# RWKV projection: GpSimd makes the low parts of the odd mixed rows, and mixed rows have four buffers instead of two

## The chip, the cores and the metric

One core of one Trainium2 chip runs the whole program. The metric is the device time of one execution in microseconds; of several executions the median is given.

## The reference

One inference step of a four-layer decoder with D = 1024, for a prompt of 512 tokens and 8 samples of 8 tokens (576 token columns in all). The mixers of the layers are RWKV-7, forgetting attention, a short convolution, and RWKV-7 again; each is followed by a convolutional FFN. The part that matters is the head of the RWKV mixer: six mixtures of the normed row and the row before it, each multiplied by a weight matrix.

```python
x_prev = jnp.concatenate([shift[:, None].astype(xn.dtype), xn[:, :-1]], axis=1)
dx = x_prev - xn
mix = lambda c: xn + dx * mu[c]
r = mix(0) @ w_rkv[0]
k = mix(2) @ w_rkv[1]
v = mix(3) @ w_rkv[2]
w_log = -jax.nn.softplus(-(w0 + jnp.tanh(mix(1) @ w1) @ w2).astype(f32)) - 0.5
iclr = jax.nn.sigmoid((a0 + (mix(4) @ a1) @ a2).astype(f32))
g = jax.nn.sigmoid(mix(5) @ g1) @ g2
```

## The kernel before

Activations lie transposed: 128 channels on the partitions, 576 token columns; the 1024 channels are 8 such rows. A matrix product is made in three matmuls with operands split into a high part (fp32r) and a low part: high times high, low times high weight, high times low weight (L408 to L410, `chunk_mm`). A chunk is 8 rows of one output tile: 8 rows x 2 halves of 288 columns x 3 = 48 matmuls.

Weights come in chunks by DMA from the queue of SyncE into four `raw` buffers. ScalarE copies a chunk to its high part `wh` (`split_hi`, L383) as soon as TensorE is done with the chunk two before; VectorE subtracts for the low part `wl` (`split_lo`, L390). Both have two buffers.

In an RWKV layer (layers 0 and 3) the mixed rows are made on the way. The projections stand in `MIX` in the order r, k, v (8 chunks each), g1, w1, a1 (one chunk each). For each of the six, a set of 8 rows is made:

- VectorE makes the mixed row `xt` = `dx` * mu + `xn` (L764, "mix" below). `xt` has two buffers, so row k waits until row k-2 has its low part.
- ScalarE copies `xt` to the high part `xh` (L779). It waits until TensorE has used this row of the set before (semaphore `a_row`).
- VectorE subtracts `xt` - `xh` into the low part `xl` (L758, "low part" below).

On VectorE the order is mix 0, mix 1, low 0, mix 2, low 1, and so on to mix 7, low 6, low 7 (`mix_rows_dve`). `mixes` (L781) puts the set of the next projection ahead of the last chunk of the present one: on VectorE and ScalarE the set comes first, then the weight split for the chunk after the next, then ScalarE's copy of the finished tile out of PSUM. TensorE (`mix_pe`, L839) waits in the first chunk of a projection, row by row, for the count of `s_xl`.

Engines run their instructions in the order written; semaphores hold them to each other. GpSimd does nothing in this stretch: its program for the layer (`a_pool`, L1717) begins with a wait for the last projection, after which `rwkv` runs the recurrence. There GpSimd's subtractions and products (L1188 to L1197, L1650) run beside VectorE's (L962, L964, L1097, L1102); in the FFN GpSimd copies a few columns (L635) beside VectorE's L390 and L595.

The address range of `xt` starts at `misc`, where the FFN has its `gate` and `conv` buffers and the recurrence its own.

Of the kernel before, what the change touches and what calls it, by code (L numbers as in the profile page):

```python
# [13 lines left out]
F32 = mybir.dt.float32  # L14
F32R = mybir.dt.float32r
I32 = mybir.dt.int32
ALU = mybir.AluOpType
ACT = mybir.ActivationFunctionType
# [4 lines left out]
KD = D // P  # L23
# [3 lines left out]
T = TP + TSN  # L27
# [65 lines left out]
MIX = [("r", 0), ("k", 2), ("v", 3), ("g1", 5), ("w1", 1), ("a1", 4)]  # L93
# [21 lines left out]
def build_program(nc, I, O, mixers=MIXERS):  # L115
# [3 lines left out]
    with ctx:  # L119
        m = Map((nc.sbuf_base + 31) // 32 * 32)  # L120

        def at(name, shape, dt, offset):
            return nc.alloc_sbuf_tensor_at(name, [P] + list(shape), dt, offset=offset)

        def sb(name, shape, dt=F32):
            return at(name, shape, dt, m.take(4 * int(np.prod(shape))))

        def sem(name):
            return ctx.enter_context(nc.semaphore(name))
# [4 lines left out]
        xh, xl = sb("xh", [KD, T], F32R), sb("xl", [KD, T], F32R)  # L134
# [4 lines left out]
        par = sb("par", [NPAR])  # L139
# [8 lines left out]
        misc = f.at  # L148
# [6 lines left out]
        co = at("co", [KF, 2 + 2 * NS], F32, f.take(4 * KF * (2 + 2 * NS)))  # L155
        cs = at("cs", [KF, 2 * NS], F32, f.take(4 * KF * 2 * NS))
        rs2 = at("rs2", [T], F32, f.take(4 * T))
        assert f.at <= nc.sbuf_usable_end, (f.at, nc.sbuf_usable_end)
        xt = at("xt", [2, T], F32, misc)

        b = Map(big)
# [31 lines left out]
        def flat3(t):  # L194
# [6 lines left out]
        xn, dx = at("xn", [KD, T], F32, at_xn), at("dx", [KD, T], F32, at_dx)  # L201
        la = at("la", [T], F32, at_rstd)
        sg = at("sg", [T], F32, a.take(4 * T))
# [10 lines left out]
        zz, csum, pprev, pinv, kraw, kn = (  # L214
            at("a_" + k, [n, NCK, CT], F32, a1.take(4 * n * TP)) for k, n in
            (("zz", 2), ("csum", 1), ("pprev", 1), ("pinv", 1), ("kraw", 1), ("kn", 1)))
# [33 lines left out]
        def pst(b, lo=0, hi=T):  # L250
            return ps[:, tile_cols(b) + lo:tile_cols(b) + hi]
# [9 lines left out]
        s_xt, s_xh, s_xl = sem("s_xt"), sem("s_xh"), sem("s_xl")  # L261
# [13 lines left out]
                "vu nc nx nb sex src ptp pts vs pn stp ogs oxh oxl").split())  # L275

        (a_ld, a_xn, a_dx, a_sh, a_w2, a_z, a_k1, a_k2, a_zz, a_kn, a_sg, a_cs, a_cm, a_kr, a_kv, a_kk, a_ex,
         a_kh, a_bb, a_ar, a_bk, a_rk, a_bo, a_bon, a_p1, a_cx, a_xe, a_cu, a_ue, a_cs2, a_s, a_co, a_oe,
         a_m, a_e, a_d, a_qx, a_qxt, a_qX, a_qxb, a_qU, a_qus, a_qo, a_qvq, a_quq, a_qs, a_qad, a_qmu,
         a_g, a_gd, a_gb, a_gc, a_gs, a_gq, a_gr, a_gl, a_ge, a_gt, a_ga, a_gh, a_kb, a_row, a_out) = (  # L280
            sem("a_" + k) for k in (
                "ld xn dx sh w2 z k1 k2 zz kn sg cs cm kr kv kk ex kh bb ar bk rk bo bon p1 cx xe cu ue cs2 s co oe "
                "m e d qx qxt qX qxb qU qus qo qvq quq qs qad qmu "
                "g gd gb gc gs gq gr gl ge gt ga gh kb row out").split())

# [4 lines left out]
        plan, c, n = {}, 0, 0  # L290
# [3 lines left out]
        for layer, (kind, idx) in enumerate(mixers):  # L294
# [10 lines left out]
            for name, nch, ntile in names:  # L305
                ph = Ph()
# [8 lines left out]
                c, n = c + nch, n + ntile  # L315
        NCHUNK = c
        n_norm, row0, raw_norm, in_place = {}, {}, {}, {}
# [29 lines left out]
        def turns(n):  # L347

            return n // 2 + 1
# [41 lines left out]
                              ALU.subtract).then_inc(s_lo, 1)  # L391

        def chunk_mm(pe, c, n, rh, rl, k0=0, nk=CH, first=True, last=True, i=0, cstep=0, nstep=0, row_ready=None,
                     row_used=None, between=None):

            pe.wait_ge(s_lo, i * cstep + c + 1)
            if first:
                pe.wait_ge(s_ev[n % 2], i * (nstep // 2) + turns(n))
            for k in range(nk):
                if between is not None:  # L400
                    between(k)
                if row_ready is not None:
                    pe.wait_ge(row_ready[0], row_ready[1] + k)
                for a in range(2):
                    out = pst(n % 2, a * HT, (a + 1) * HT)
                    rhs_h, rhs_l = rh[:, k0 + k, a * HT:(a + 1) * HT], rl[:, k0 + k, a * HT:(a + 1) * HT]
                    w_h, w_l = wh[:, c % SPL, k], wl[:, c % SPL, k]
                    pe.matmul(out, w_h, rhs_h, start=(first and k == 0), stop=False)  # L408
                    pe.matmul(out, w_h, rhs_l, start=False, stop=False)  # L409
                    mm = pe.matmul(out, w_l, rhs_h, start=False, stop=(last and k == nk - 1))  # L410
                if row_used is not None and k < nk - 1:
                    mm.then_inc(row_used, 1)
            mm.then_inc(s_mm, 1)
# [130 lines left out]
        def first_chunk(pe, c, n, q, e):  # L544

            def between(k):
                if k == CH // 2:
                    last_squares(pe, q - 1)

            chunk_mm(pe, c, n, xh, xl, row_ready=(s_gl, KD * e + 1), between=between)  # L550
# [201 lines left out]
        def mix_rows_dve(dve, layer, j, n):  # L752

            r0 = row0[layer, "mix"] + n * KD

            def lo(k):
                dve.wait_ge(s_xh, r0 + k + 1)
                dve.tensor_tensor(xl[:, k], xt[:, k % 2], xh[:, k].bitcast(F32), ALU.subtract).then_inc(s_xl, 1)  # L758

            for k in range(KD):  # L760
                if k >= 2 or n:
                    dve.wait_ge(s_xl, r0 + k - 1)
                mu = PC["mu", j] + MIX[n][1] * KD + k
                dve.scalar_tensor_tensor(xt[:, k % 2], dx[:, k], par[:, mu:mu + 1], xn[:, k],  # L764
                                         ALU.mult, ALU.add).then_inc(s_xt, 1)
                if k >= 1:
                    lo(k - 1)
            lo(KD - 1)

        def mix_rows_act(act, layer, j, n):  # L770
            r0 = row0[layer, "mix"] + n * KD
            for k in range(KD):
                act.wait_ge(s_xt, r0 + k + 1)
                if n and k < KD - 1:
                    act.wait_ge(a_row, ((len(MIX) - 1) * j + n - 1) * (KD - 1) + k + 1)
                elif n:
                    before = plan[layer, MIX[n - 1][0]]
                    act.wait_ge(s_mm, before.c0 + before.nch)
                act.activation(xh[:, k], xt[:, k % 2], ACT.Copy).then_inc(s_xh, 1)  # L779

        def mixes(eng, layer, j, mix_rows, chunk):  # L781

# [46 lines left out]
        def key_squares(pe, j, k):  # L829

            pe.wait_ge(a_k2, KD * j + k + 1)
            for blk in range(5):
                at_ = 16 * blk + 2 * k
                for h in range(2 if blk < 4 else 1):
                    mm = pe.matmul(bank(7)[64 * h:64 * h + 64, at_:at_ + 2],
                                   sq[:, k % 2, blk * P + 64 * h:blk * P + 64 * h + 64], hs2(), start=True, stop=True)
            mm.then_inc(a_kn, 1)

        def mix_pe(pe, layer, j, n):  # L839
            name = MIX[n][0]  # L840
            ph = plan[layer, name]
            r0 = row0[layer, "mix"] + n * KD
            for k in range(ph.nch):
                chunk_mm(pe, ph.c0 + k, ph.n0 + k, xh, xl, row_ready=(s_xl, r0 + 1) if k == 0 else None,
                         row_used=a_row if k == ph.nch - 1 and n + 1 < len(MIX) else None)
                if name == "k" and k:
                    key_squares(pe, j, k - 1)
                if name == "v" and k == 0:
                    key_squares(pe, j, KD - 1)
# [40 lines left out]
        def after(eng, s, v):  # L890

            if v > 0:
                eng.wait_ge(s, v)
# [3 lines left out]
        t3, bb, kh = zz0, zz1, kn  # L897
# [279 lines left out]
        def prep_pool(pool, B, G, k):  # L1177
# [36 lines left out]
            k=("et", "m6", 2, "copy", "", "m1", ("p16", "vst")),  # L1214
# [270 lines left out]
        def rwkv(eng, j, inv_step, chain_part, prep_piece, first, seq, states_in=None):  # L1485

            fns = (inv_step, chain_part, prep_piece)
            for k in range(NPREP):
                prep_piece(eng, Bat(j, 0), None, k)
            first(eng, Bat(j, 0))  # L1490
            for c in range(KD + 1):
                half(eng, *fns, Bat(j, c), Bat(j, c - 1) if c else None, Bat(j, c + 1) if c < KD else None,
                     Bat(j, c - 2) if c >= 2 else None, states_in if c == KD - 1 else None)
            seq(eng, j, Bat(j, KD, 7))
# [220 lines left out]
            res_dve(dve, plan[layer, "out"], 1, norm_behind(layer, "out"), None, True)  # L1715

        def a_pool(pool, layer, j):  # L1717
            pool.wait_ge(s_mm, plan[layer, MIX[-1][0]].c0 + 1)
            pool.wait_ge(a_ld, 64 * (j + 1))
            rwkv(pool, j, inv_pool, no_chain, prep_pool, first_none, seq_pool)  # L1720
# [912 lines left out]
```

## Time and profile before

| | before |
|---|---|
| median of three runs | 3803.13 us (3798.8 to 3804.16) |
| profiled execution | 3803.17 us, its span 3801.3 us |
| busy share of the span | TensorE 95%, weight loads 89%, VectorE 48%, ScalarE 37%, GpSimd 11% |
| TensorE's granted clock, mean | 0.975 of full speed |

PE is TensorE's matmuls, PEld its weight loads, DVE is VectorE, ACT ScalarE, POOL GpSimd, SP SyncE. A row of a timeline has the start in us from the start of the span, the duration in us, then engine, line, operation, out<-in and shape; like neighbours are merged (x2). In brackets stands how long the engine was idle before and which instruction ended that. Matmuls are pipelined: one starts before the end of the one ahead, so the pace is read from the starts.

### The profile page before, as it was taken

What the parts mean: (1) busy time and instruction counts of PE and PEld (TensorE: products, weight loads), DVE (VectorE), ACT (ScalarE), POOL (GpSimd) and SP (SyncE); (2) the same over time, 40 slices, a digit from 0 to 9 for tenths busy, and PEclk for the clock granted to TensorE, in tenths of its full rate; (3) what the DMA queues carried; (4) which work ended last, traced back from release to release, by engine and by line L of the source; (5) the groups of instructions that cost most, each with busy time, mean ns of one, the idle gap of its engine ahead of it and who ended that gap; (6) DMA issues with size and microseconds to landing.
All of it is one profiled execution on the core that took longest, in us unless ns stands there. A gap on an engine that the chain in (4) does not pass through costs nothing.

```text
span 3801.3 us, 95974 instructions
## 1 busy us (share of the span) xinstructions
PE 3598.1 (95%) x41213; PEld 3367.6 (89%) x41213; DVE 1830.8 (48%) x2739; ACT 1403.5 (37%) x2390; POOL 424.3 (11%) x570
## 2 busy tenths in 40 slices
PE   6979989999999989899999999999798899999999
PEld 5968888999999955699999999999798787899999
DVE  3465544555245644355533445552435655455532
ACT  2345542444222533244422224442234454244421
POOL 0012211111000000011100101110000332211100
PEclk8989989999999999999999999999899899999999
DMA  3210001222222378422222222222222000122222
GB/s 121 73 45 4 4 25 67 83 83 84 79 83 80 115 281 301 162 82 81 83 86 84 84 73 85 79 81 86 87 73 67 14 4 26 38 80 83 83 81 80
DMA packets 95940, 314.75 MB, mean 83 GB/s; under 512 B 18946, under 2 KB 20226, under 8 KB 94866
## 3 DMA queue, kind: packets, MB, share of 16 engines
q1 hardware_dynamic: 87410, 285.25, 22.5%
q10 hardware_dynamic: 8224, 24.88, 1.7%
q8 instruction: 257, 4.21, 0.5%
q14 instruction: 49, 0.40, 0.0%
HBM read 297.30 MB, written 12.79 MB: 82 GB/s over the span
## 4 chain that ended last, share of the span: by engine, by line
PE 88%; DVE 6%; ACT 3%; issue 2%; DMA 0%; POOL 0%; ACTq 0%; SPq 0%; DVEq 0%; POOLq 0%
PE ps L408 22%; PE ps L410 22%; PE ps L409 22%; PE ps L1342 6%; DVE xt L764 2%; PE ps L538 2%; DVE xl L758 1%; PE ps L904 1%; PE ps L461 1%; PE ps L1421 1%; PE ps L1911 1%; PE ps L1512 1%; PE ps L2010 1%; PE ps L1946 1%; PE ps L1966 1%
## 5 line engine op out<-in xcount | busy, mean ns | idle before, releaser
L408 PE MATMUL ps<-xh,wh 128*128 128x288 f32 x4720 | 1418.5, 301 | 67.6 <-DVE xl L758 66.8
L409 PE MATMUL ps<-xl,wh 128*128 128x288 f32 x4720 | 1397.4, 296 | 0.0
L410 PE MATMUL ps<-xh,wl 128*128 128x288 f32 x4720 | 1392.5, 295 | 0.0
L408 PEld LDWEIGHTS ps<-xh,wh 128*128 128x128 f32 x4720 | 889.1, 188 | 83.0 <-issue 51.2
L383 ACT ACTIVATE wh<-raw 128x1024 fp32r<-128x1024 f32 x415 | 439.2, 1058 | 1249.4 <-PE ps L410 1241.2
L410 PEld LDWEIGHTS ps<-xh,wl 128*128 128x128 f32 x4720 | 893.5, 189 | 0.0
L409 PEld LDWEIGHTS ps<-xl,wh 128*128 128x128 f32 x4720 | 891.6, 189 | 2.0
L390 DVE TENSOR_TENSOR wl<-raw,wh 128x1024 fp32r<-128x1024 f32 x415 | 508.3, 1225 | 611.1 <-ACT wh L383 608.5
L408 PE MATMUL ps<-hh,wh 128*128 128x288 f32 x1536 | 464.5, 302 | 0.0
L410 PE MATMUL ps<-hh,wl 128*128 128x288 f32 x1536 | 457.0, 298 | 0.0
L409 PE MATMUL ps<-hl,wh 128*128 128x288 f32 x1536 | 450.0, 293 | 0.0
L409 PEld LDWEIGHTS ps<-hl,wh 128*128 128x128 f32 x1536 | 294.5, 192 | 2.0
L408 PEld LDWEIGHTS ps<-hh,wh 128*128 128x128 f32 x1536 | 290.5, 189 | 2.8 <-issue 0.7
L410 PEld LDWEIGHTS ps<-hh,wl 128*128 128x128 f32 x1536 | 289.8, 189 | 0.0
L1342 PE MATMUL ps<-m,m 64*64 64x64 f32 x5952 | 238.4, 224 | 14.0 <-issue 7.5
L1342 PEld LDWEIGHTS ps<-m,m 64*64 64x64 f32 x5952 | 202.4, 136 | 50.0 <-issue 44.2
L635 POOL COPY co<-gate 128x2 f32 x96 | 113.9, 1186 | 1046.9 <-DVE gate L448 916.0
L448 DVE TENSOR_TENSOR gate<-ps,rstd 128x512 f32<-128x512 f32 (+1 forms) x176 | 72.5, 454 | 293.1 <-PE ps L410 291.8
L492 ACT ACTIVATE sq<-x 128x576 f32<-128x576 f32 (+1 forms) x64 | 44.0, 687 | 341.9 <-DVE x L509 160.8
L1361 ACT ACTIVATE m<-ps 128x256 f32<-128x256 f32 x272 | 105.6, 389 | 132.4 <-PE ps L1342 128.8
L509 DVE TENSOR_TENSOR x<-x,ps 128x576 f32<-128x576 f32 (+1 forms) x64 | 48.3, 754 | 201.0 <-PE ps L410 201.0
L448 DVE TENSOR_TENSOR conv<-conv,rstd 128x512 f32<-128x512 f32 x192 | 79.5, 456 | 67.8 <-ACT conv L578 67.5
(333 smaller groups left out, 4870.7 us busy)
## 6 DMA issues: line engine op xcount, KB each, us to landing
raw<-in_w SPq DMA_DIRECT2D x415, 512.0 KB, 3.4
kp<-in_cache_k SPq DMA_DIRECT2D x64, 512.0 KB, 5.7
vp<-in_cache_v SPq DMA_DIRECT2D x64, 512.0 KB, 5.8
rkv<-in_wkv ACTq DMA_DIRECT2D x2, 2048.0 KB, 10.0
out_wkvs<-rkv ACTq DMA_DIRECT2D x2, 2048.0 KB, 7.2
x<-in_x ACTq DMA_DIRECT2D x1, 2304.0 KB, 13.0
out_k<-qk ACTq DMA_DIRECT2D x1, 2304.0 KB, 7.0
out_v<-vg ACTq DMA_DIRECT2D x1, 2304.0 KB, 13.0
```

Source lines behind the costliest of these rows:

```text
L383: act.activation(wh[:, c % SPL], raw[:, c % RAWS], ACT.Copy).then_inc(s_hi, 1)
L390: dve.tensor_tensor(wl[:, c % SPL], raw[:, c % RAWS], wh[:, c % SPL].bitcast(F32), ALU.subtract).then_inc(s_lo, 1)
L408: pe.matmul(out, w_h, rhs_h, start=(first and k == 0), stop=False)
L409: pe.matmul(out, w_h, rhs_l, start=False, stop=False)
L410: mm = pe.matmul(out, w_l, rhs_h, start=False, stop=(last and k == nk - 1))
L448: op = dve.tensor_tensor(out(part), src(part), tok(r, part), ALU.mult)
L509: dve.tensor_tensor(row, row, pst(n % 2).rearrange("p (o t) -> p o t", o=1), ALU.add)\
L538: mm = pe.matmul(pst(STAT, a * HT, (a + 1) * HT), ones, sq[:, (j + 1) % 2, a * HT:(a + 1) * HT], start=False, stop=False)
L635: pool.tensor_copy(co[:, bass.ds(i * 2 + u, 1), 0:2], one(gate[:, u, GS - 2:GS]))
L764: dve.scalar_tensor_tensor(xt[:, k % 2], dx[:, k], par[:, mu:mu + 1], xn[:, k], ALU.mult, ALU.add).then_inc(s_xt, 1)
L1342: mm = pe.matmul(bank(bk + part)[to, at_:at_ + CT], operand(B, left, p)[r], mview("ist")[r] if right == "ist" else operand(B, right, p)[r] ...
L1361: act.activation(sl[to][:, of], half_of(bk, part), ACT.Copy).then_inc(a_e, 1)
```

## The change

GpSimd makes the low parts of rows 1, 3, 5 and 7 of each set and counts them on a new semaphore `a_xo`; VectorE makes those of rows 0, 2, 4 and 6 and counts them on `s_xl`. VectorE's order is now mix 0, mix 1, low 0, mix 2, mix 3, low 2, and so on to mix 6, mix 7, low 6. `xt` has four buffers, so mix k waits for the low part of row k-4, of whichever engine. TensorE waits for each row on the semaphore of the engine that makes it.

```diff
-        xt = at("xt", [2, T], F32, misc)
+        xt = at("xt", [4, T], F32, misc)
...
         def chunk_mm(pe, c, n, rh, rl, k0=0, nk=CH, first=True, last=True, i=0, cstep=0, nstep=0, row_ready=None,
-                     row_used=None, between=None):
+                     row_used=None, between=None, mixed=None):
...
+                if mixed is not None:
+                    pe.wait_ge((s_xl, a_xo)[k % 2], mixed // 2 + k // 2 + 1)
...
             def lo(k):
                 dve.wait_ge(s_xh, r0 + k + 1)
-                dve.tensor_tensor(xl[:, k], xt[:, k % 2], xh[:, k].bitcast(F32), ALU.subtract).then_inc(s_xl, 1)
+                dve.tensor_tensor(xl[:, k], xt[:, k % 4], xh[:, k].bitcast(F32), ALU.subtract).then_inc(s_xl, 1)
 
             for k in range(KD):
-                if k >= 2 or n:
-                    dve.wait_ge(s_xl, r0 + k - 1)
+                if k % 2:
+                    after(dve, a_xo, r0 // 2 + k // 2 - 1)
+                else:
+                    after(dve, s_xl, r0 // 2 + k // 2 - 1)
                 mu = PC["mu", j] + MIX[n][1] * KD + k
-                dve.scalar_tensor_tensor(xt[:, k % 2], dx[:, k], par[:, mu:mu + 1], xn[:, k],
+                dve.scalar_tensor_tensor(xt[:, k % 4], dx[:, k], par[:, mu:mu + 1], xn[:, k],
                                          ALU.mult, ALU.add).then_inc(s_xt, 1)
-                if k >= 1:
+                if k % 2:
                     lo(k - 1)
-            lo(KD - 1)
+
+        def mix_rows_pool(pool, layer, j, n):
+
+            r0 = row0[layer, "mix"] + n * KD
+            for k in range(1, KD, 2):
+                pool.wait_ge(s_xh, r0 + k + 1)
+                pool.tensor_tensor(xl[:, k], xt[:, k % 4], xh[:, k].bitcast(F32), ALU.subtract).then_inc(a_xo, 1)
...
-                act.activation(xh[:, k], xt[:, k % 2], ACT.Copy).then_inc(s_xh, 1)
+                act.activation(xh[:, k], xt[:, k % 4], ACT.Copy).then_inc(s_xh, 1)
...
-                chunk_mm(pe, ph.c0 + k, ph.n0 + k, xh, xl, row_ready=(s_xl, r0 + 1) if k == 0 else None,
+                chunk_mm(pe, ph.c0 + k, ph.n0 + k, xh, xl, mixed=r0 if k == 0 else None,
                          row_used=a_row if k == ph.nch - 1 and n + 1 < len(MIX) else None)
...
         def a_pool(pool, layer, j):
+            for n in range(len(MIX)):
+                mix_rows_pool(pool, layer, j, n)
             pool.wait_ge(s_mm, plan[layer, MIX[-1][0]].c0 + 1)
```

## Rows read from the trace of the kernel before

**Rows 1.** the page's costliest groups: line, engine, operation | busy us, mean ns | idle before

```profile
L408 PE MATMUL ps<-xh,wh 128*128 128x288 f32 x4720 | 1418.5, 301 | 67.6 <-DVE xl L758 66.8
```

**Rows 2.** TensorE's waits, 37 to 262 and 2720 to 2965 us: total, times, longest

```profile
PE ps L408 <- DVE xl L758: 33.1, 24, 18.9
...
PE ps L408 <- DVE xl L758: 33.7, 23, 19.8
```

**Rows 3.** timeline of TensorE at 224 to 232 us: start us, us, instruction

```profile
224.76 0.29 PE L409 MATMUL ps<-xl,wh 128*128 128x288 f32 x1
224.90 0.29 PE L410 MATMUL ps<-xh,wl 128*128 128x288 f32 x1
227.87 0.37 PE L408 MATMUL ps<-xh,wh 128*128 128x288 f32 x1 [2.69 <-DVE xl L758]
```

**Rows 4.** timeline of VectorE, the set of projection g1

```profile
211.77 1.54 DVE L764 SCALAR_TENSOR_TENSOR xt<-dx,par,xn 128x576 f32<-128x576 f32 x2
213.34 0.76 DVE L758 TENSOR_TENSOR xl<-xt,xh 128x576 fp32r<-128x576 f32 x1
214.13 0.82 DVE L764 SCALAR_TENSOR_TENSOR xt<-dx,par,xn 128x576 f32<-128x576 f32 x1
214.87 0.75 DVE L758 TENSOR_TENSOR xl<-xt,xh 128x576 fp32r<-128x576 f32 x1
...
222.48 1.59 DVE L758 TENSOR_TENSOR xl<-xt,xh 128x576 fp32r<-128x576 f32 x2
224.26 1.23 DVE L390 TENSOR_TENSOR wl<-raw,wh 128x1024 fp32r<-128x1024 f32 x1 [0.19 <-ACT wh L383]
```

**Rows 5.** timeline of ScalarE, the same set

```profile
212.62 1.42 ACT L779 ACTIVATE xh<-xt 128x576 fp32r<-128x576 f32 x2 [1.49 <-DVE xt L764]
...
223.19 1.04 ACT L383 ACTIVATE wh<-raw 128x1024 fp32r<-128x1024 f32 x1
```

**Rows 6.** stretch of one set: length, busy PE PEld DVE ACT POOL, clock, DMA, GB/s

```profile
225.40:239.00 13.60, 9.31 (x48) 7.78 (x48) 13.09 (x18) 7.57 (x10) 0.00 (x0) 0.87 0.11 39
```

**Rows 7.** timeline of VectorE at 281 us, in the recurrence

```profile
280.81 0.68 DVE L1097 SCALAR_TENSOR_TENSOR a_kn<-a_zz,rkv 128x512 f32<-128x512 f32 x1
...
281.74 1.42 DVE L1102 SCALAR_TENSOR_TENSOR a_zz<-rkv,par,a_kn 128x512 f32<-128x512 f32 x1
```

**Rows 8.** timeline of GpSimd over the same stretch

```profile
280.97 1.65 POOL L1191 TENSOR_TENSOR a_zz<-a_kraw,a_zz 128x512 f32<-128x512 f32 x1 [3.48 <-DVE a_kraw L1090]
282.70 1.59 POOL L1195 TENSOR_TENSOR bst<-a_zz,a_pinv 128x512 f32<-128x512 f32 x1
284.25 1.27 POOL L1197 TENSOR_TENSOR kst<-a_kn,a_pinv 128x512 f32<-128x512 f32 x1
```

**Rows 9.** lines L964 and L962: duration in ns, least, median, most

```profile
L964 DVE TENSOR_TENSOR rkv<-rkv x18: 691/693/1520, 535.6 to 3294.2; 128x512 f32<-128x512 f32 x18
...
L962 DVE TENSOR_TENSOR rkv<-rkv,ps x18: 677/686/689, 534.9 to 3293.5; 128x512 f32<-128x512 f32 x18
```

**Rows 10.** timeline at 581 us, VectorE's L964 and GpSimd's L1650

```profile
580.98 1.52 DVE L964 TENSOR_TENSOR rkv<-rkv 128x512 f32<-128x512 f32 x1
...
580.91 1.04 POOL L1650 TENSOR_TENSOR uq<-a_kraw,msk 128x512 f32<-128x512 f32 x1
...
581.91 1.49 POOL L1650 TENSOR_TENSOR uq<-a_kraw,msk 128x512 f32<-128x512 f32 x1
```

**Rows 11.** timeline of the FFN at 710 us

```profile
709.52 1.23 DVE L390 TENSOR_TENSOR wl<-raw,wh 128x1024 fp32r<-128x1024 f32 x1 [0.18 <-ACT wh L383]
...
709.58 1.21 POOL L635 COPY co<-gate 128x2 f32 x1 [10.66 <-DVE gate L448]
...
710.66 0.83 DVE L595 SCALAR_TENSOR_TENSOR conv<-gate,par,conv 128x592 f32<-128x592 f32 x1
```

**Rows 12.** GpSimd's first subtraction (line L1188) and the timeline before it

```profile
L1188 POOLq MODIFY_POOL_CONFIG  x2: 6/6/6, 252.8 to 252.9; - x2
...
258.05 1.36 POOL L1188 TENSOR_TENSOR a_pprev<-a_csum,a_zz 128x512 f32<-128x512 f32 x1 [5.16 <-DVE a_csum L1070]
```

More of the change, by code:

```diff
@@ L277, in build_program @@
         (a_ld, a_xn, a_dx, a_sh, a_w2, a_z, a_k1, a_k2, a_zz, a_kn, a_sg, a_cs, a_cm, a_kr, a_kv, a_kk, a_ex,
-         a_kh, a_bb, a_ar, a_bk, a_rk, a_bo, a_bon, a_p1, a_cx, a_xe, a_cu, a_ue, a_cs2, a_s, a_co, a_oe,
+         a_kh, a_bb, a_ar, a_bk, a_xo, a_rk, a_bo, a_bon, a_p1, a_cx, a_xe, a_cu, a_ue, a_cs2, a_s, a_co, a_oe,
          a_m, a_e, a_d, a_qx, a_qxt, a_qX, a_qxb, a_qU, a_qus, a_qo, a_qvq, a_quq, a_qs, a_qad, a_qmu,
@@ L281, in build_program @@
             sem("a_" + k) for k in (
-                "ld xn dx sh w2 z k1 k2 zz kn sg cs cm kr kv kk ex kh bb ar bk rk bo bon p1 cx xe cu ue cs2 s co oe "
+                "ld xn dx sh w2 z k1 k2 zz kn sg cs cm kr kv kk ex kh bb ar bk xo rk bo bon p1 cx xe cu ue cs2 s co oe "
                 "m e d qx qxt qX qxb qU qus qo qvq quq qs qad qmu "
```

## The prediction

> **What bounds the kernel now.** I read the page's costliest groups first: TensorE is the long engine, and in front of L408, the first matmul of a row, it stands idle for 67.6 us, of which the waits for `xl` of L758 are 66.8 us [rows 1]. Then TensorE's waits in the two stretches that hold the change, one for each RWKV layer: 33.1 and 33.7 us [rows 2]. The longest of each, 18.9 and 19.8 us, is the norm ahead of the first row, which the change doesn't touch. So 14.2 and 13.9 us remain, and these rows count less than what is lost: a matmul is recorded as 0.29 us but starts 0.13 us after the one before [rows 3], so a row of six takes 0.80 us, a chunk of 48 matmuls 6.4 us.
>
> The timeline of VectorE shows why there is a wait. In one set (eight rows) VectorE runs mix, low part, mix, low part without a pause: 213.34 to 214.87 is one row, 1.52 us, against TensorE's 0.80. Counted from its first mix (211.77), a set ends its last low part at 12.30 us, and the weight split behind it at 13.72 us [rows 4]. ScalarE, with 0.7 us a row, follows [rows 5]. Three of the six projections have one chunk only, and there one set follows on the other every 13.6 us while TensorE needs 6.4. Such a set begins with a wait of TensorE, 2.69 us at 227.87 [rows 3], and in such a stretch the granted clock is 0.87 of full speed [rows 6]: part of it runs at the lower of the two levels. That costs little, as TensorE waits for rows anyway.
>
> **The change part by part.** *Removed:* 4 of 16 VectorE instructions per set, 48 of the 96 low parts, each 0.75 us. *Added:* 48 GpSimd subtractions of 128x576, no new DMA, and a wait of VectorE on GpSimd's row k-4.
>
> If VectorE and GpSimd did not disturb each other, a pair of rows would cost VectorE 0.73 + 0.73 + 0.75 = 2.2 us and some wait instead of 3.04. But they do. GpSimd's L1191 started at 280.97, in VectorE's L1097 (280.81 to 281.49), and ended at 282.62, 1.13 us after the end of L1097. VectorE's L1102, issued at 281.74, ended 0.54 us after that, at 283.16. GpSimd's L1195, started at 282.70, ended 1.13 us later still [rows 7, 8]. One after the other, then: whoever comes second does nothing until the first has ended. An undisturbed one took 1.27 us [rows 8]. The same VectorE line shows both prices: L964, with two SBUF operands, takes 693 ns, and 1520 ns where it meets GpSimd; L962, with one operand in PSUM, never takes over 689 ns [rows 9]. There GpSimd's operation ended at 581.95, L964 at 582.50, and GpSimd's next, begun at 581.91, took 1.49 us instead of 1.04 [rows 10]. Mix (`dx`, `xn`), low part (`xt`, `xh`) and weight split (`raw`, `wh`) all read two SBUF tensors. I take the exclusion as holding for all of them.
>
> Price of one GpSimd subtraction: no row has 576 columns. By columns (576/512 = 1.125) the hold is 1.13 x 1.125 = 1.27 us, and an undisturbed one 1.43 us. Bounds: below, 0.90 us (L1650 from 582.50 to 583.40, with a broadcast operand [rows 10]) x 1.125 = 1.02; above, the whole 1.65 us of L1191 [rows 8] x 1.125 = 1.86, should writing fp32r cost GpSimd more. I take 1.27, as L1191 and L1195 have the same two full operands. VectorE's rest after a release is 0.54 x 1.125 = 0.61.
>
> Who gets in first? In the FFN, GpSimd's L635, of two columns, waited from 709.58 through VectorE's split (709.52 to 710.75) and was done at 710.79, ahead of VectorE's L595, issued at 710.66 [rows 11]. So GpSimd gets its turn between two VectorE instructions.
>
> Now one set, from its first mix at 0 (ScalarE 0.69 us per high part): mix 0 to 0.82, mix 1 to 1.55, low 0 to 2.33, mix 2 from 2.25 to 3.06. Row 1's high part is ready at 2.28, only 0.05 us ahead of the turn at 2.33; I let GpSimd miss it, get the one at 3.06 and hold to 4.33 (if it gets the first, the walk below gives 10 us a layer, 3823). Mix 3, held back, ends at 4.94; low 2 runs from 4.86. From here each pair repeats: mix 0.73, GpSimd 1.27, rest of a mix 0.61, low 0.67 = 3.28 us a pair, against 3.04 now. Low 6 ends at about 12.3; low 7, on GpSimd from 12.3 and undisturbed, at 13.7, 1.4 us later than now. ScalarE's weight part is ready by 13.4, but VectorE's split now waits for low 7: 13.7 + 1.08 = 14.8, 1.1 us later than now. Each set delays TensorE by one or the other, so a layer loses between 6 x 1.1 = 6.6 and 6 x 1.43 = 8.6 us. Walking the four queues set by set gave 1.5, 1.5, 0.9, 1.4, 1.0 and 1.0: 7.3. Two layers: **+14.5 us**.
>
> Costed at nothing: the four buffers. A mix now starts 0.035 us behind the low part it waits for (213.34 + 0.76 to 214.13 [rows 4]); with four it waits for row k-4, done a pair before, and the 0.035 is in the pairs above. If row k-4's part on GpSimd is late, mix k stands, with VectorE's later low parts and weight splits queued behind. TensorE's wait per row in place of a count: nothing. GpSimd's own queue: its copy for the recurrence comes behind the last set and wants the last projection anyway. GpSimd's first subtraction brings two MODIFY_POOL_CONFIG of 6 ns, which stood at 252.8, ahead of a wait that ended at 258.05, not behind it [rows 12]; they will now stand at the program's start, under 40 us of idle. Were they behind the wait, up to 5.2 us once. The lower clock: a row takes 1.6 us at half speed, against 1.64 between rows, so at most some tenths at each set's last row, under 4 us in all, in the range.
>
> Sum against the profiled execution: its own time is 3803.17 us (span 3801.3), and the median of the three runs is 3803.13, the same. 3803.2 + 14.5 = 3817.7, say 3818.
>
> **The rivals.** *No exclusion for these operations* (faster). The place is VectorE's pair of rows: 2.24 us, GpSimd's 1.43 beside it. The same walk ends the last low part at 10.5 instead of 12.3 and the weight split at 11.4 instead of 13.7, 1.8 to 2.35 us a set, 12.5 a layer: 3803 - 25 = 3778. For it: no row shows a mix beside a GpSimd operation. Against: the same kinds of instruction do exclude each other [rows 7 to 10]. The point that decides is the hold of GpSimd: 0.73 + hold + 0.61 + 0.67 = 3.04 at 1.03 us; below it, faster.
>
> The Trainium skill, Advanced Engine Details and Errata, Mode Summary, notes the blocking only for GpSimd against VectorE instructions in a two-port mode, and the Trainium skill, VectorE: DVE Perf Modes, The perf-mode tier table, gives fp32 `tensor_tensor` no such mode; by that the time would be the 3778 of this rival. The GPSIMD Details of the first page count VectorE instructions with two SBUF inputs in as well, and the 1520 ns are on the side of this second line.
>
> *A short hold.* Each us of hold is worth 24 us a layer (24 pairs): at 1.02 it is 7.3 - 24 x 0.25 = 1.3 a layer, 3806: no change that can be measured.
>
> *GpSimd is slower at fp32r.* At 1.86 us: 7.3 + 24 x 0.59 = 21.5 a layer, 3846. Against: the hold of 1.13 repeats to 0.01 in rows 7 and 8.
>
> **How the numbers follow.** Exclusion with a hold of about 1.1 to 1.5: 0.60, 3810 to 3830, likeliest 3818. Short hold, 3803 to 3810: 0.13. Slow GpSimd, 3830 to 3846: 0.09. No exclusion, about 3778: 0.18. About 0.2% (7.6 us) is what a measurement here can tell from no change. Faster 0.18, same 0.13, slower 0.69. The range, 3802 to 3846, leaves out the case of no exclusion and little else, 0.2.
>
> **What would show it.** Right: VectorE's mixes and low parts fall into two durations, undisturbed (0.75 to 0.82) and about 1.9 to 2.0 us for the mix that meets GpSimd; GpSimd's subtractions take 1.4 to 2.0 us, the wait in them included; a set lasts about 13.7 us to its last low part; TensorE's waits name `xl` of GpSimd. Wrong: mixes that stay at 0.82 us beside GpSimd, sets of 10.5 us, or a GpSimd hold below 1.03 us; a first set later by some 5 us would mean the configuration is behind the wait.

## The result, and the profile after

| | before | after |
|---|---|---|
| median of nine runs each | 3802.77 us (3798.8 to 3804.16) | 3813.11 us (3806.32 to 3820.27) |
| ratio of the times | 1 | 1.003, 95% interval 1.0022 to 1.0039 |
| profiled execution, its span | 3803.17 us, 3801.3 us | 3814.71 us, 3812.9 us |
| TensorE's granted clock, mean | 0.975 | 0.977 |

The changed kernel is slower by 0.2 to 0.4%: 8.4 to 14.8 us by the interval, 10.3 by the medians, 11.5 between the two profiled executions. The lines moved a little: mix is now L768, VectorE's low part L760, GpSimd's L778, ScalarE's high part L789, the first matmul of a row L410.

The page, first the busy shares of the engines, then the groups that answer to [rows 1] (busy us, mean ns | idle time before and what ended it):

```profile
PE 3599.5 (94%) x41213; PEld 3363.0 (88%) x41213; DVE 1837.6 (48%) x2691; ACT 1403.1 (37%) x2390; POOL 508.5 (13%) x618
...
L410 PE MATMUL ps<-xh,wh 128*128 128x288 f32 x4720 | 1422.4, 301 | 75.6 <-DVE xl L760 52.0
...
L778 POOL TENSOR_TENSOR xl<-xt,xh 128x576 fp32r<-128x576 f32 x48 | 86.0, 1792 | 563.4 <-ACT xh L789 563.4
```

VectorE has 48 instructions fewer for the low parts and still 48% of the span: what it gave away it spends blocked. TensorE stands idle before the first matmul of a row for 75.6 us, 8.0 more than in [rows 1]. In the first of the two stretches (37 to 266 us) its waits now have two names:

```profile
PE ps L410 <- DVE xl L760: 25.6, 12, 18.9
PE ps L410 <- POOL xl L778: 11.3, 16, 0.9
```

Beside the norm's 18.9 that is 6.7 + 11.3 = 18.0 us, against 14.2 in [rows 2].

The cause stands in the set of one projection with one chunk. VectorE's timeline (start, us, instruction), answering to [rows 4]:

```profile
232.15 1.53 DVE L768 SCALAR_TENSOR_TENSOR xt<-dx,par,xn 128x576 f32<-128x576 f32 x2
233.71 0.76 DVE L760 TENSOR_TENSOR xl<-xt,xh 128x576 fp32r<-128x576 f32 x1
234.38 2.69 DVE L768 SCALAR_TENSOR_TENSOR xt<-dx,par,xn 128x576 f32<-128x576 f32 x2
237.00 0.75 DVE L760 TENSOR_TENSOR xl<-xt,xh 128x576 fp32r<-128x576 f32 x1
237.67 2.70 DVE L768 SCALAR_TENSOR_TENSOR xt<-dx,par,xn 128x576 f32<-128x576 f32 x2
...
245.36 1.60 DVE L390 TENSOR_TENSOR wl<-raw,wh 128x1024 fp32r<-128x1024 f32 x1 [1.03 <-ACT wh L383]
246.88 1.53 DVE L768 SCALAR_TENSOR_TENSOR xt<-dx,par,xn 128x576 f32<-128x576 f32 x2
```

GpSimd's timeline over the same set:

```profile
234.48 1.98 POOL L778 TENSOR_TENSOR xl<-xt,xh 128x576 fp32r<-128x576 f32 x1 [3.34 <-ACT xh L789]
237.88 1.88 POOL L778 TENSOR_TENSOR xl<-xt,xh 128x576 fp32r<-128x576 f32 x1 [1.41 <-ACT xh L789]
241.17 1.87 POOL L778 TENSOR_TENSOR xl<-xt,xh 128x576 fp32r<-128x576 f32 x1 [1.42 <-ACT xh L789]
244.46 1.42 POOL L778 TENSOR_TENSOR xl<-xt,xh 128x576 fp32r<-128x576 f32 x1 [1.41 <-ACT xh L789]
```

The first two mixes meet nobody: 1.53 us for two. The next two take 2.69. The first of these runs from 234.38 to 235.19, GpSimd's subtraction is let in at its end and holds until 236.46 (234.48 + 1.98), and the second mix, issued at 235.11, ends only at 237.07, 0.61 behind that. The pair repeats every 3.29 us (234.38 to 237.67), against 3.04 before. The fourth subtraction meets nobody and takes 1.42. The set's last low part ends at 245.88, 13.73 us after the set's first mix (12.30 in [rows 4]), and the split behind it, held until then, is done at 246.96, 14.81 us after that mix (13.72 before). The same set as one window (length, then busy us of TensorE, weight loads, VectorE, ScalarE and GpSimd, clock, DMA share, GB/s), answering to [rows 6]:

```profile
232.15:246.90 14.75, 10.58 (x49) 8.96 (x48) 13.70 (x15) 7.98 (x11) 7.15 (x4) 0.77 0.12 36
```

VectorE is occupied for 13.70 of 14.75 us. The granted clock is 0.77, against 0.87 in [rows 6]: more of the stretch, in which TensorE waits row by row, runs at the lower level of 1.2 GHz. TensorE's timeline shows a wait within a set and the one at the start of the next, answering to [rows 3]:

```profile
245.93 0.40 PE L410 MATMUL ps<-xh,wh 128*128 128x288 f32 x1 [0.49 <-POOL xl L778]
...
249.34 0.58 PE L410 MATMUL ps<-xh,wh 128*128 128x288 f32 x1 [2.36 <-DVE xl L760]
```

The wait at the start of the set is shorter than the 2.69 of [rows 3], but its matmuls are recorded as 0.40 to 0.58 us where 0.29 is usual. Slower matmuls fill part of what would otherwise be waiting, so the recorded waits grew by less than the time did: in the stage defined below TensorE is busy for 195.6 us per layer, 191.9 before, with the same 1440 matmuls.

Over both layers, the mixes and low parts of the kernel before (minimum, median, maximum in ns), then those of the changed kernel and the pool configuration that GpSimd's line brings:

```profile
L764 DVE SCALAR_TENSOR_TENSOR xt<-dx,par,xn x96: 810/818/821, 43.5 to 2951.6; 128x576 f32<-128x576 f32 x96
...
L758 DVE TENSOR_TENSOR xl<-xt,xh x96: 748/751/761, 45.1 to 2953.1; 128x576 fp32r<-128x576 f32 x96
```

```profile
L768 DVE SCALAR_TENSOR_TENSOR xt<-dx,par,xn x96: 804/812/1997, 45.2 to 2960.7; 128x576 f32<-128x576 f32 x96
...
L760 DVE TENSOR_TENSOR xl<-xt,xh x48: 744/746/760, 46.7 to 2962.6; 128x576 fp32r<-128x576 f32 x48
L778 POOL TENSOR_TENSOR xl<-xt,xh x48: 1414/1872/2017, 47.5 to 2963.5; 128x576 fp32r<-128x576 f32 x48
...
L778 POOLq MODIFY_POOL_CONFIG  x2: 11/11/11, 0.8 to 0.8; - x2
```

For what follows I call **stage** the time from the start of a layer's first mix to the start of its last projection matmul, read from the timelines. It holds all that the change touches.

| | us per layer | against before |
|---|---|---|
| before | 208.61 | |
| after | 216.29 | +7.68 |

### The profile page after: what moved, and what is told of

Read it like the earlier page. It is cut to its first block, busy times and chain, and to the rows that moved or that the text cites. A ratio compares the mean times of both kernels' runs of the same rounds, so it can differ in the third digit from the quotient of the medians.

```text
span 3812.9 us, 95975 instructions
## 1 busy us (share of the span) xinstructions
PE 3599.5 (94%) x41213; PEld 3363.0 (88%) x41213; DVE 1837.6 (48%) x2691; ACT 1403.1 (37%) x2390; POOL 508.5 (13%) x618
## 4 chain that ended last, share of the span: by engine, by line
PE 88%; DVE 6%; ACT 3%; issue 2%; POOL 1%; DMA 0%; ACTq 0%; SPq 0%; DVEq 0%; POOLq 0%
PE ps L410 22%; PE ps L412 22%; PE ps L411 22%; PE ps L1352 6%; DVE xt L768 3%; PE ps L540 2%; PE ps L914 1%; PE ps L463 1%; PE ps L1923 1%; PE ps L1431 1%; DVE xl L760 1%; PE ps L1958 1%; PE ps L1522 1%; PE ps L1033 1%; PE ps L930 1%
## 5 line engine op out<-in xcount | busy, mean ns | idle before, releaser
L410 PE MATMUL ps<-xh,wh 128*128 128x288 f32 x4720 | 1422.4, 301 | 75.6 <-DVE xl L760 52.0
L410 PEld LDWEIGHTS ps<-xh,wh 128*128 128x128 f32 x4720 | 891.4, 189 | 96.3 <-issue 49.8
L410 PE MATMUL ps<-hh,wh 128*128 128x288 f32 x1536 | 463.9, 302 | 0.0
L410 PEld LDWEIGHTS ps<-hh,wh 128*128 128x128 f32 x1536 | 289.6, 189 | 2.7 <-issue 0.7
L1352 PE MATMUL ps<-m,m 64*64 64x64 f32 x5952 | 237.6, 224 | 14.8 <-issue 8.1
L778 POOL TENSOR_TENSOR xl<-xt,xh 128x576 fp32r<-128x576 f32 x48 | 86.0, 1792 | 563.4 <-ACT xh L789 563.4
```

Of the source, the lines that this page charges most:

```text
L778: pool.tensor_tensor(xl[:, k], xt[:, k % 4], xh[:, k].bitcast(F32), ALU.subtract).then_inc(a_xo, 1)
L1352: mm = pe.matmul(bank(bk + part)[to, at_:at_ + CT], operand(B, left, p)[r], mview("ist")[r] if right == "ist" else operand(B, right, p)[r] ...
```

## The experiments

Two theories stood against each other. **Exclusion**: a GpSimd elementwise instruction and a VectorE instruction that reads two SBUF tensors run one after the other, never together. **Something else**: VectorE's longer set comes from the new order and the new waits, or from the buffers. The runs of e1 to e4 were compared with one set of runs of before (median 3802.65 us), those of e5 to e7 with another (3801.38).

| run | median us | ratio, 95% interval | stage against before, us per layer |
|---|---|---|---|
| e1_buffers | 3795.39 | 0.9981 (0.9971 to 0.999) | -4.46 |
| e2_beside | 3859.92 | 1.0151 (1.0136 to 1.0167) | +29.0, +28.0 |
| e3_beside_copy | 3819.63 | 1.0045 (1.003 to 1.0061) | +8.70 |
| e4_ahead | 3776.99 | 0.9936 (0.9922 to 0.9949) | -11.87 |
| e5_two | 3827.95 | 1.0069 (1.0052 to 1.0086) | +11.86 |
| e6_odd_sbuf | 3827.04 | 1.0066 (1.0049 to 1.0083) | +14.04 |
| e7_odd_psum | 3801.06 | 0.9995 (0.9986 to 1.0005) | -0.17 |

**e1_buffers: the four buffers alone.** The kernel before, with no GpSimd.

```diff
-        xt = at("xt", [2, T], F32, misc)
+        xt = at("xt", [4, T], F32, misc)
...
-                if k >= 2 or n:
-                    dve.wait_ge(s_xl, r0 + k - 1)
+                if k >= 4 or n:
+                    dve.wait_ge(s_xl, r0 + k - 3)
```

> Only the four buffers of the mixed rows; every low part stays on VectorE, in the order of the kernel before. Theory A (a mix that need not wait for the low part just ahead of it starts 0.085 us before that one's end instead of 0.035 us after): a row drops from 1.52 to about 1.40 us, a set to its last low part from 12.30 to about 11.5, a layer by about 4.3 us, the time to about 3794. Then the GpSimd part of the change costs some 12 us a layer, not 7.7, and the buffers hide a part of it. Theory B, the prediction's (the buffers are worth nothing by themselves): 3803, a set of 12.3.

VectorE's timeline of one set:

```profile
211.67 0.76 DVE L758 TENSOR_TENSOR xl<-xt,xh 128x576 fp32r<-128x576 f32 x1
212.34 0.81 DVE L764 SCALAR_TENSOR_TENSOR xt<-dx,par,xn 128x576 f32<-128x576 f32 x1
213.07 0.75 DVE L758 TENSOR_TENSOR xl<-xt,xh 128x576 fp32r<-128x576 f32 x1
213.74 0.81 DVE L764 SCALAR_TENSOR_TENSOR xt<-dx,par,xn 128x576 f32<-128x576 f32 x1
```

A row takes 1.40 us (211.67 to 213.07) instead of 1.52. Before, a mix waited for the low part directly ahead of it on its own engine and started 0.03 us after that one's end (213.34 + 0.76 = 214.10, and 214.13 [rows 4]); now it waits for an older low part and starts 0.09 us ahead of that end (211.67 + 0.76 = 212.43, and 212.34). The set ends its last low part at 11.55 us instead of 12.30. So the buffers by themselves make the kernel faster, by 4.46 us a layer. The wait and the place of the row change together here; that the wait is what costs the 0.12 us is argued from the gap, and no run has the one without the other.

**e2_beside: GpSimd's work added, nobody waits for it.** The kernel before with two buffers; per set GpSimd makes four subtractions of `dx` and `xn` into two rows that nothing reads. This is extra work; the output doesn't depend on it.

```diff
+            for k in range(1, KD, 2):
+                pool.wait_ge(s_xh, r0 + k + 1)
+                after(pool, a_xo, r0 // 2 + k // 2 - 1)
+                pool.tensor_tensor(xt[:, 2 + k // 2 % 2], dx[:, k], xn[:, k], ALU.subtract).then_inc(a_xo, 1)
```

> The kernel before, and beside it four GpSimd subtractions of 128x576 in each set, at the times at which the changed kernel has its own, from two rows that don't change (dx, xn) into two rows that nothing reads; nobody in the set waits for them. Theory A (GpSimd and VectorE exclude each other while both read two SBUF tensors): each costs VectorE its hold of about 1.27 us less what falls into pauses, a set of about 16.5 us instead of 12.3, 25 us a layer, 3853. Theory B (the changed kernel lost because the low parts of GpSimd come late, not because VectorE is held up): 3803, VectorE's mixes and low parts unchanged at 0.82 and 0.75 us.

The tile `xt` and one weight split:

```profile
L764 DVE SCALAR_TENSOR_TENSOR xt<-dx,par,xn x96: 804/819/2030, 44.7 to 3009.1; 128x576 f32<-128x576 f32 x96
...
L758 DVE TENSOR_TENSOR xl<-xt,xh x96: 744/756/1978, 46.3 to 3010.6; 128x576 fp32r<-128x576 f32 x96
L776 POOL TENSOR_TENSOR xt<-dx,xn x48: 1412/1988/2003, 47.0 to 3010.7; 128x576 f32<-128x576 f32 x48
```

```profile
245.31 2.16 DVE L390 TENSOR_TENSOR wl<-raw,wh 128x1024 fp32r<-128x1024 f32 x1 [0.19 <-ACT wh L383]
```

VectorE's order and waits are those of before, and nothing in the set waits for GpSimd; still mixes and low parts last up to 2.0 us, and the time rises by 57 us. So the loss needs neither the new order nor a new wait. Nor do the two instructions need a tensor in common: the low parts read `xt` and `xh`, GpSimd `dx` and `xn`. It is more than the 25 us a layer that I had expected: in a set with one chunk the fourth subtraction, from 244.40 us, also holds the weight split, 2.16 us instead of the 1.23 of [rows 4]. TensorE's clock has a part in it too: it was 0.80 from 183 to 200 us, where projection v starts; the same part of before has 1.00 (168 to 182 us).

**e3_beside_copy: the same with one SBUF operand on GpSimd.** Four copies of `dx` per set in place of the subtractions, again read by nothing.

```diff
-                pool.tensor_tensor(xt[:, 2 + k // 2 % 2], dx[:, k], xn[:, k], ALU.subtract).then_inc(a_xo, 1)
+                pool.tensor_copy(xt[:, 2 + k // 2 % 2], dx[:, k]).then_inc(a_xo, 1)
```

> As the run before, but GpSimd copies 128x576 (one SBUF operand) into the rows that nothing reads. 
The tile `xt`:

```profile
L764 DVE SCALAR_TENSOR_TENSOR xt<-dx,par,xn x96: 805/819/1244, 44.5 to 2965.6; 128x576 f32<-128x576 f32 x96
...
L758 DVE TENSOR_TENSOR xl<-xt,xh x96: 743/756/1222, 46.0 to 2967.2; 128x576 fp32r<-128x576 f32 x96
L776 POOL COPY xt<-dx x48: 664/1262/1276, 46.8 to 2967.2; 128x576 f32<-128x576 f32 x48
```

The copy, undisturbed 0.66 us, waits and makes wait just as the subtraction does. On GpSimd's side one operand is enough, and the shorter instruction costs less: 8.7 us a layer here, 28.5 with the subtraction.

**e5_two: the change with two buffers.**

```diff
-        xt = at("xt", [4, T], F32, misc)
+        xt = at("xt", [2, T], F32, misc)
...
-                    after(dve, a_xo, r0 // 2 + k // 2 - 1)
+                    after(dve, a_xo, r0 // 2 + k // 2)
...
-                    after(dve, s_xl, r0 // 2 + k // 2 - 1)
+                    after(dve, s_xl, r0 // 2 + k // 2)
```

> The changed kernel with two buffers of the mixed rows in place of four: GpSimd's part alone. Theory A (GpSimd's turns hold VectorE, and the buffers hide a part of it): mix k must now wait for the low part of row k-2 as well, by the same walk of the queues 12 us a layer over the kernel before, 3827; with the four buffers it was 7.7. Theory B (the buffers do nothing in the changed kernel): 3813, like the changed kernel.

GpSimd's part, with the order and the waits that come with it, costs 11.86 us a layer, and the buffers give back 4.18 of them (11.86 - 7.68), nearly the 4.46 of e1_buffers.

**e6_odd_sbuf and e7_odd_psum: only the place of one buffer differs.** Both start from the changed kernel and take the rows in the order 1, 0, 3, 2 and so on, so that VectorE's low part of an even row meets GpSimd's of an odd one. In e6 the even mixed rows lie in SBUF, in e7 in PSUM; both have one buffer for even rows and two for odd ones.

```diff
+        def xrow(k):
+            return xt[:, 1 + k // 2 % 2] if k % 2 else xt[:, 0]
...
-            for k in range(KD):
+            for k in (1, 0, 3, 2, 5, 4, 7, 6):
```

In e7 the one line differs:

```diff
-            return xt[:, 1 + k // 2 % 2] if k % 2 else xt[:, 0]
+            return xt[:, 1 + k // 2 % 2] if k % 2 else ps[:, 2048:2048 + T]
```

> The changed kernel with another order on VectorE, mix 1, mix 0, low 0, mix 3, mix 2, low 2 and so on, so that GpSimd's low part falls beside VectorE's low part and not beside a mix; one buffer for the even mixed rows, two for the odd, all in SBUF. Theory A: VectorE's low parts read two SBUF tensors too, so they are held up in their turn (about 1.35 us in place of 0.75), a pair of rows takes 3.7 us: 14 us a layer over the kernel before, 3832. Theory B (only a mix with its three operands is held up): as the next run, about 3805.

> As the run before, instruction for instruction, but the buffer of the even mixed rows lies in PSUM, so that VectorE's low parts read one SBUF tensor and one PSUM tensor. Theory A (two SBUF operands make the exclusion): VectorE's low parts run beside GpSimd's at 0.75 us, a pair takes about 2.97 us: 1 us a layer over the kernel before, 3805. Theory B (the exclusion is one of the engines, whatever VectorE reads): 3832, as the run before.

The low parts of the two engines in e6 (ns, minimum, median, maximum):

```profile
L780 POOL TENSOR_TENSOR xl<-xt,xh x48: 1397/1412/1446, 45.7 to 2976.6; 128x576 fp32r<-128x576 f32 x48
L773 DVE TENSOR_TENSOR xl<-xt,xh x48: 1328/1342/1381, 46.4 to 2977.2; 128x576 fp32r<-128x576 f32 x48
```

A pair of them in e6, first VectorE's timeline, then GpSimd's:

```profile
222.41 1.38 DVE L773 TENSOR_TENSOR xl<-xt,xh 128x576 fp32r<-128x576 f32 x1 [0.75 <-ACT xh L791]
```

```profile
221.73 1.45 POOL L780 TENSOR_TENSOR xl<-xt,xh 128x576 fp32r<-128x576 f32 x1 [45.73 <-ACT xh L791]
```

The same in e7:

```profile
215.34 0.76 DVE L773 TENSOR_TENSOR xl<-ps,xh 128x576 fp32r<-128x576 f32 x1 [0.72 <-ACT xh L791]
216.01 0.81 DVE L769 SCALAR_TENSOR_TENSOR xt<-dx,par,xn 128x576 f32<-128x576 f32 x1
```

```profile
214.68 1.44 POOL L780 TENSOR_TENSOR xl<-xt,xh 128x576 fp32r<-128x576 f32 x1 [45.13 <-ACT xh L791]
```

In e6 every low part of VectorE takes 1.33 to 1.38 us. The one shown begins inside GpSimd's subtraction and ends at 223.79, 0.61 us behind that one's end (223.18). In e7 the same instruction begins and ends inside GpSimd's (214.68 to 216.12) and takes 0.76; GpSimd's takes 1.44, hardly more than undisturbed. The place of the buffer also changes where the mix writes and where ScalarE reads, but those hardly differ: a mix into PSUM takes 0.82 us and one into SBUF 0.81, ScalarE's copy 0.65 and 0.69. With the same order, waits and number of buffers the two kernels lie 26 us apart (3827.04 and 3801.06). So what excludes is two SBUF operands on VectorE's side, not the fact that both engines work. e7 is no faster than before either: in its order VectorE waits 0.72 us for ScalarE in every pair.

The Trainium skill, SBUF — State Buffer, Who interferes with whom, says this: VectorE and GpSimd share a pair of SBUF ports as an exclusive lock, held for a whole instruction, and a VectorE instruction with two SBUF inputs contends for it with a GpSimd instruction that reads SBUF, while one with a single SBUF input, outside the two-port modes, doesn't. The traces agree: 1.34 us with two (e6), 0.76 with one (e7), and a GpSimd copy, which reads one tensor, is enough (e3). That page excepts GpSimd instructions that only write; no run here has one.

**e4_ahead: no GpSimd, the work moved into VectorE's idle time.** Four buffers as in e1; ahead of an eight-chunk projection's end, the first four mixed rows of the next set are made one chunk earlier, ahead of the weight split there; the other four follow between the low parts.

```diff
+            if part != 1:
+                for k in range(4):
+                    mix(k)
+            if part == 0:
+                return
+            for k in range(KD):
+                lo(k)
+                if 1 <= k < 5:
+                    mix(k + 3)
...
+                    early = mix_rows is mix_rows_dve and ph.nch > 1
+                    if early and k == ph.nch - 2:
+                        mix_rows(eng, layer, j, n + 1, 0)
```

> No GpSimd part. Four buffers, and VectorE makes the first four mixed rows of the next set one chunk earlier where the present projection has eight chunks, in a stretch in which it is idle some 5 us a chunk; then low 0, low 1, mix 4, low 2 and so on. Theory (VectorE's instructions between the end of the last chunk but one and the last low part are what TensorE waits for): 12 us a layer less, 3803 - 24 = 3779. Rival (TensorE waits for ScalarE's high parts, which wait for rows to be used): nothing beyond the buffers, 3794.

VectorE's timeline, then TensorE's waits for rows in the first stretch (40 to 285 us):

```profile
91.66 3.00 DVE L764 SCALAR_TENSOR_TENSOR xt<-dx,par,xn 128x576 f32<-128x576 f32 x4
96.91 1.23 DVE L390 TENSOR_TENSOR wl<-raw,wh 128x1024 fp32r<-128x1024 f32 x1 [2.25 <-ACT wh L383]
98.06 1.42 DVE L758 TENSOR_TENSOR xl<-xt,xh 128x576 fp32r<-128x576 f32 x2
...
104.32 2.08 DVE L758 TENSOR_TENSOR xl<-xt,xh 128x576 fp32r<-128x576 f32 x3
```

```profile
PE ps L408 <- DVE xl L758: 27.1, 5, 20.3
```

Four mixes run while VectorE would have been idle, and it still waits 2.25 us for the next split. Then the first two low parts are done within 1.42 us. TensorE waits 5 times instead of 24, 6.8 us beside the norm's wait (here 20.3) instead of 14.2 [rows 2]. This kernel beats both: it is faster than before by 0.5 to 0.8%. Of its 11.87 us a layer the four buffers alone are worth 4.46 (e1); 7.41 are left for the order.

## Why the prediction was right, and which step of it was not

The forecast was 3818 us, the range 3802 to 3846, slower with 0.69. It came out at 3813.11, slower by more than the 0.2% named there, with the whole interval (1.0022 to 1.0039) beyond it.

**The exclusion** was read from other instructions of the kernel [rows 7 to 10] and taken to hold for mix and low part. It does: shown in the changed kernel, and told apart from order, waits and buffers by e1, e2, e6 and e7. The rival without exclusion, 3778, would have had mixes that stay at 0.82 us; they go up to 1.997. Of the two lines that the prediction set against each other (the Trainium skill, Advanced Engine Details and Errata, Mode Summary and GPSIMD Details), the runs agree with the second, which counts VectorE instructions with two SBUF inputs in: a mix that meets GpSimd takes 1.96 us (235.11 to 237.07).

**The prices** taken by columns were right almost to the last digit: hold 1.27 us forecast and 1.27 measured (235.19 to 236.46), rest of a held mix 0.61 and 0.61, an undisturbed subtraction 1.43 and 1.42, a pair of rows 3.28 and 3.29. That GpSimd misses the first turn was assumed and not derived, and by the prediction's own walk it is worth 2.7 us a layer (10 against 7.3), so a part of the agreement is luck. It did miss it in all 12 sets, by 0.1 us: in the set shown mix 2 is recorded from 2.23 us and the first subtraction from 2.33. In e5, where mix 2 must wait for low 0 and is recorded from 2.35, GpSimd comes first and takes 1.41. One slip in the bounds changes nothing: 0.90 x 1.125 is 1.01, not 1.02.

**The set and the layer**: last low part at 13.7 forecast and 13.73 measured, split done at 14.8 and 14.81, layer +7.3 and +7.68. The configuration of GpSimd stands at 0.8 us, under idle time, as forecast. The layer is only 0.4 us above a sum that held nothing for the lower clock; so it cost little, as forecast, unless another term hides it.

**The step that failed** is "Costed at nothing: the four buffers". They are worth 4.46 us a layer by themselves (e1) and 4.18 in the changed kernel (e5). The net came out right because the walk of the changed kernel used starts ahead of the end of the instruction before, as in 0.67 for a low part, while the text gave the buffers no price: it named the 0.035 us behind a low part, but what goes with the wait is 0.12 us per row (1.52 to 1.40), the gap and the overlap together. So the change is a loss of 11.86 us a layer and a gain of 4.18, and the gain would have been worth having alone. No rival named that.

**The size**: two layers give 15.4 us in the stage of the profiled executions, the forecast 14.5, the medians 10.3 (8.4 to 14.8). The profiled executions show where they differ: from the last projection matmul of the first RWKV layer to the first mix of the second, before took 2493.97 us and after 2487.99, 6.0 less; ahead of the first stage and behind the second after has 1.6 and 0.5 us more, so 15.4 + 1.6 - 6.0 + 0.5 gives 11.5, that of the profiled executions. That piece holds nothing that the change edits. TensorE's clock accounts for most of it: over the same matmuls TensorE is busy for 2396.4 us in before and 2391.7 in after, 4.7 less, and the granted clock is at the lower level for 97.5 us of the piece in before and for 87.3 in after. So it is in the other runs: e2 has 95 us at the lower level and takes 2494.3 us, the other six have 84 to 88 and take 2488.7 to 2490.8. One stretch of it is 491 to 499 us in before, with a clock of 0.57, where after has 1.00 (499 to 507 us). Why the clock fell more often in those two executions stays open.

## What to carry to other kernels

Before handing elementwise work to GpSimd, look at what VectorE runs at that moment: beside VectorE instructions that read two SBUF tensors it costs VectorE its full hold (here 1.27 us to save 0.75), and it held up nothing beside one that had an operand in PSUM. A VectorE wait for its own instruction just ahead went with 0.12 us on every row here, so another buffer can pay where the profile shows no idle time at all. First move the work into the engine's own idle time one step earlier: here that and the four buffers gave 26 us, 18 more than the buffers alone, where the second engine with the same buffers cost 10.

## What was unexpected of the hardware

- A copy with one SBUF operand on GpSimd excludes VectorE's two-operand instructions as well: they last up to 1.24 us beside it instead of 0.82 (e3).
- GpSimd loses next to no time to a VectorE instruction with a PSUM operand: 1.40 to 1.44 us beside one (e7), 1.41 to 1.43 undisturbed (the fourth subtraction of a set in the changed kernel).
- With a wait for VectorE's own preceding instruction, and the shared buffer behind it, the next starts 0.12 us later than without, 0.03 us behind that one's end and not 0.09 ahead of it (before against e1).
